# A hybrid decoder layer: recurrent rows first in the output projection, decay operands made during the input tiles, and the third down remainder behind the hidden halves

## The reference, cut to what matters

```python
h = x + concat(GatedDeltaNet(u), RG_LRU(u)) @ w_out      # u = rmsnorm(x); one projection u @ w_in feeds both
h = h + CrossAttn(rmsnorm(h), rmsnorm(mem))              # 4 heads, 256 memory tokens
h = h + MoE(rmsnorm(h))                                  # top 4 of 32 clamped-SwiGLU experts, D_FF = 1024
out = rmsnorm(h)

# GatedDeltaNet, 4 heads of 128: gcum = cumsum(g); decay = exp(gcum_t - gcum_s) below the diagonal
o = rmsnorm(o, dn_norm) * silu(z)                        # per head, then into the output projection
# one expert, for its tokens:
gt = min(x @ w_gate + b_gate, 7); up = clip(x @ w_up + b_up, -7, 7)
hid = (up + 1) * (gt * sigmoid(1.702 * gt)); y = hid @ w_down + b_down
```

## Time and profile before

| | us |
|---|---|
| median of three runs | 1742.11 |
| lowest, highest run | 1738.88, 1742.91 |
| profiled execution | 1739.81 |
| its span, first to last instruction | 1738.1 |

### The profile page before, as it was taken

How to read it: one execution, slowest core, us unless ns; L and a number is a source line. 1 busy time by engine, 2 the same in 40 slices (tenths; PEclk the granted TensorE clock), 3 DMA queues, 4 the chain that set the end, 5 groups by cost and what they waited for, 6 DMA issues and landing times.

```text
span 1738.1 us, 24427 instructions
## 1 busy us (share of the span) xinstructions
PE 1664.3 (96%) x8001; PEld 1367.4 (79%) x8001; DVE 1435.6 (83%) x1546; ACT 1273.5 (73%) x1456; POOL 496.4 (29%) x569
## 2 busy tenths in 40 slices
PE   5999899899899999999999999999999999999996
PEld 3778598787768888888888888888888888888885
DVE  3558796663348999999999999999999999999997
ACT  4554474454445788888888888888888888888885
POOL 3354461200023422223232232222322222222223
PEclk9999999999999999999999999999999999999999
DMA  7212200052024999999999999999999999999992
GB/s 253 103 37 93 84 1 2 25 194 97 8 102 194 375 363 383 380 355 384 362 385 383 353 376 368 382 380 356 369 376 379 375 364 363 379 381 361 375 355 107
DMA packets 53385, 476.19 MB, mean 274 GB/s; under 512 B 9991, under 2 KB 11144, under 8 KB 28770
## 3 DMA queue, kind: packets, MB, share of 16 engines
q1 hardware_dynamic: 42000, 450.69, 64.0%
q0 software_dynamic: 11152, 24.92, 6.3%
q10 hardware_dynamic: 194, 0.06, 0.0%
HBM read 461.24 MB, written 23.08 MB: 279 GB/s over the span
## 4 chain that ended last, share of the span: by engine, by line
PE 63%; DVE 16%; issue 13%; ACT 6%; POOL 1%; DMA 0%; ACTq 0%; DVEq 0%; POOLq 0%
PE ps L1569 19%; PE ps L1527 18%; PE ps L1147 10%; DVE wsp L1920 6%; PE ps L1318 4%; PE ps L1554 2%; ACT extra L1052 2%; PE ps L1502 2%; DVE extra L2109 1%; DVE extra L2107 1%; DVE wsp_b L1920 1%; DVE wf L1639 1%; PE ps L1252 1%; PE ps L1240 1%; PE ps L1409 1%
## 5 line engine op out<-in xcount | busy, mean ns | idle before, releaser
L1920 DVE TENSOR_TENSOR wsp<-ring,wsp 128x1024 fp32r<-128x1024 f32 x512 | 600.8, 1221 | 32.2 <-ACT wsp L1007 32.1
L1007 ACT ACTIVATE wsp<-ring 128x1024 fp32r<-128x1024 f32 x388 | 386.8, 1053 | 68.7 <-PE ps L1513 53.4
L589 POOL TENSOR_TENSOR guard<-guard 1x1 f32<-1x1 f32 x190 | 127.4, 670 | 772.3 <-ACT extra L1075 309.0
L1527 PE MATMUL ps<-wsp,x_hi 128*128 128x512 f32 x1152 | 308.1, 389 | 0.0
L1920 DVE TENSOR_TENSOR wsp_b<-ring,wsp_b 128x1024 fp32r<-128x1024 f32 x256 | 301.7, 1221 | 0.0
L1527 PEld LDWEIGHTS ps<-wsp,x_hi 128*128 128x128 f32 x1152 | 216.1, 188 | 45.7 <-issue 0.5
L1007 ACT ACTIVATE wsp_b<-ring 128x1024 fp32r<-128x1024 f32 x194 | 202.3, 1059 | 24.7 <-PE ps L1527 12.0
L1527 PE MATMUL ps<-wsp,x_lo 128*128 128x512 f32 x576 | 177.5, 389 | 0.0
L1639 DVE TENSOR_TENSOR wf<-ring,wf 128x1024 fp32r<-128x1024 f32 x64 | 81.3, 1273 | 106.0 <-ACT wf L707 106.0
L707 ACT ACTIVATE wf<-ring 128x1024 fp32r<-128x1024 f32 x80 | 84.3, 1056 | 112.0 <-PE ps L1147 62.5
L1147 PE MATMUL ps<-act_hi,wf 128*128 128x512 f32 x512 | 161.5, 397 | 2.6 <-DVE wf L1639 2.0
(11 more groups left out here) (382 smaller groups left out, 2951.9 us busy)
## 6 DMA issues: line engine op xcount, KB each, us to landing
ring<-in_w_gate_dram SPq DMA_DIRECT2D x32, 4096.0 KB, 15.0
ring<-in_w_up_dram SPq DMA_DIRECT2D x32, 4096.0 KB, 13.9
ring<-in_w_down_dram SPq DMA_DIRECT2D x32, 4096.0 KB, 13.0
ring<-in_w_in_dram SPq DMA_DIRECT2D x6, 2048.0 KB, 12.5
ring<-in_w_ckv_dram SPq DMA_DIRECT2D x4, 2048.0 KB, 10.2
ring<-in_w_out_dram SPq DMA_DIRECT2D x2, 2048.0 KB, 10.5
ring<-in_w_cq_dram SPq DMA_DIRECT2D x2, 2048.0 KB, 10.0
ring<-in_w_co_dram SPq DMA_DIRECT2D x2, 2048.0 KB, 10.0
```

Of the source, the lines that this page charges most:

```text
L589: return pool.tensor_tensor(guard[:, i:i + 1], guard[:, 0:1], guard[:, 0:1], ALU.mult)
L1007: act.activation(split_w(c, 0), ring[:, m, k], ACT.Copy).then_inc(hi_ready, 1)
L1527: last = pe.matmul(ps[:, 2 * j + i], xp[:, k * P:(k + 1) * P], split_w(c, part)[:, i * 512:(i + 1) * 512], start=False, stop=(k == KT - 1 ...
L1920: dve.tensor_tensor(split_w(c, 1), ring[:, (GM + c // KT) % 3, c % KT], split_w(c, 0), ALU.subtract).then_inc(lo_ready, 1)
```

## The change

Three places change. In the output projection all eight pieces of recurrent rows come first, for all four output groups; the rounding and remainders of the pieces move with them, the norm weight goes from a GpSimd instruction of its own into VectorE's multiply, both `fill_wait` go, and SP loads the memory rows after the scan's last output. The decay operands are made behind tiles 20, 21 and 22 into `y_m`, and their matmuls wait for their own bank's tile (18 to 21); the wait for tile 24 stands behind them. In the expert blocks `lo(18)` is issued behind both hidden halves.

```diff
@@ -284,8 +284,7 @@
         F_END = F_CO + N_CO
 
 
-        OUT_ORDER = ([(0, 0, 2), (0, 0, 3), (0, 1, 2), (0, 1, 3), (0, 0, 0), (0, 0, 1), (0, 1, 0), (0, 1, 1)]
-                     + [(1, n, kp) for n in range(2) for kp in (2, 3, 0, 1)])
+        OUT_ORDER = [(tp, n, kp) for kps in ((2, 3), (0, 1)) for tp in range(2) for n in range(2) for kp in kps]
         CV_ORDER = [(0, n, kp) for n in range(2) for kp in range(4)]
         CO_ORDER = [(tp, n, kp) for tp in range(2) for n in range(2) for kp in range(4)]
 
@@ -369,7 +368,7 @@
             sp.dma_start(w_ba[:], w_in[0].rearrange("(k p) n -> p k n", p=P)[:, :, C_BA:C_BA + 2 * H]).then_inc(ba_in, 16)
             for m in range(NF):
                 if m == W_CV:
-                    sp.wait_ge(dn_done, H)
+                    sp.wait_ge(o_done, 4 * NT)
                     sp.dma_start(chan[:, 0:4, :].rearrange("p a t -> p (a t)").rearrange("p (m d) -> p m d", m=MT),
                                  mem[0].rearrange("(m p) d -> p m d", p=P)).then_inc(mem_in, 16)
                 if m in FREE:
@@ -510,7 +509,6 @@
                 link(pool.tensor_tensor(chan[:, h], chan[:, h], q_m[:, h % 2], ALU.mult))
                 pool.tensor_copy(elast[:, 4 * h:4 * h + 4].unsqueeze(2), quart(q_m[:, h % 2])[:, :, P - 1:P]).then_inc(qexp_ready, 1)
                 pool.wait_ge(kk_evac, 4 * h + 1)
-                pool.wait_ge(gb_done, H)
                 if h >= 2:
                     pool.wait_ge(x1_ready, h - 1)
                 level_mask(0, h)
@@ -536,7 +534,6 @@
 
             for h in range(H):
                 pool.wait_ge(onorm_ready, h + 1)
-                link(pool.tensor_scalar(onrm(h), onrm(h), par[:, R_DN:R_DN + 1], None, ALU.mult))
                 pool.tensor_tensor(chan[:, 12 + h], chan[:, 12 + h], onrm(h), ALU.mult).then_inc(dn_done, 1)
 
 
@@ -881,22 +878,20 @@
             for h in range(H):
                 act.wait_ge(o_done, 4 * (NT - 1) + (h + 1 if h < 2 else H))
                 act.activation(onrm(h), ps[:, 4 + h], ACT.Square).then_inc(osq_ready, 1)
+                if h >= 2:
+                    piece_hi(F_OUT + h)
                 act.wait_ge(oss_done, h + 1)
                 act.activation(onrm(h), ps[:, h % 2], ACT.Sqrt, scale=1.0 / P, bias=eps_t).then_inc(orms_ready, 1)
-            piece_hi(F_OUT + 2)
-            piece_hi(F_OUT + 3)
-
             for h in range(H):
+                for i in ((), (4, 5), (6,), (7,))[h]:
+                    piece_hi(F_OUT + i)
                 act.wait_ge(dn_done, h + 1)
                 act.activation(act_hi[:, (6, 7, 4, 5)[h]], chan[:, 12 + h], ACT.Copy).then_inc(ah_ready, 1)
-                if h == 2:
-                    piece_hi(F_OUT + 4)
-            piece_hi(F_OUT + 5)
 
 
             s = NT
             memf = chan[:, 0:4, :].rearrange("p a t -> p (a t)").rearrange("p (m d) -> p m d", m=MT)
-            for i in range(6, 4 * HALF):
+            for i in range(2 * HALF, 4 * HALF):
                 piece_hi(F_OUT + i)
                 if i in (9, 11):
                     norm_rows(memf[:, s - NT], s, [(mem_in, 16)])
@@ -1170,10 +1165,10 @@
                     pe.matmul(ps[:, 6 + i % 2], ones[:], chan[:, 16 + i], start=True, stop=True).then_inc(l2_done, 1)
 
 
-            pe.wait_ge(tile_done, 24)
             for h in range(H):
+                pe.wait_ge(tile_done, 19 + h)
                 pe.wait_ge(gu_ready, h + 1)
-                pe.matmul(ps[:, h], ones[:], as_m[:, h % 2], start=True, stop=True).then_inc(gb_done, 1)
+                pe.matmul(ps[:, h], ones[:], y_m[:, h], start=True, stop=True).then_inc(gb_done, 1)
 
 
             def rg_gates(n):
@@ -1182,6 +1177,8 @@
                     if n > 0:
                         pe.wait_ge(ri_ready, 2 * (n - 1) + g + 1)
                     pe.matmul(ps[:, g], rgw[:, g, n], chan[:, 16 + n], start=True, stop=True).then_inc(gate_mm, 1)
+
+            pe.wait_ge(tile_done, 24)
 
             def head_products(h):
 
@@ -1340,12 +1337,11 @@
                 if h == 2:
                     mixer_out(1)
             pe.wait_ge(orms_ready, H)
-            fill_wait(24, 0)
             for i in range(2, 4 * HALF):
-                if i == 4:
-                    pe.wait_ge(onorm_ready, H)
-                    fill_wait(14, 4)
-                    pe.wait_ge(al_ready, A_DN)
+                if i in (4, 6):
+                    pe.wait_ge(onorm_ready, i - 2)
+                if i in (8, 9):
+                    pe.wait_ge(al_ready, A_DN + 2 * (i - 9))
                 if i == 14:
                     for m in range(MT):
                         transposes(NT + m, 2 * m)
@@ -1718,6 +1714,11 @@
                 if j == 3:
                     dve.wait_ge(gp_done, 1)
                     dve.tensor_copy(gp, ps[:, 7, 64:80]).then_inc(gp_ready, 1)
+                for h in {20: (0, 1), 21: (2,), 22: (3,)}.get(j, ()):
+                    if h == 0:
+                        dve.wait_ge(bias_out, 16 * 4)
+                    dve.tensor_tensor(quart(y_m[:, h]), tri[:].unsqueeze(1).to_broadcast([P, 4, P]),
+                                      g_t[:, 4 * h:4 * h + 4].unsqueeze(2).to_broadcast([P, 4, P]), ALU.mult).then_inc(gu_ready, 1)
                 if 11 <= j < 19:
                     i = j - 11
                     dve.wait_ge(norm_ready, i // 4 + 1)
@@ -1725,12 +1726,6 @@
                     dve.tensor_tensor(chan[:, i], chan[:, i], chan[:, 16 + i], ALU.mult).then_inc(qk_ready, 1)
 
 
-            for h in range(H):
-                dve.wait_ge(proj_done, 24)
-                if h >= 2:
-                    dve.wait_ge(gb_done, h - 1)
-                dve.tensor_tensor(quart(as_m[:, h % 2]), tri[:].unsqueeze(1).to_broadcast([P, 4, P]),
-                                  g_t[:, 4 * h:4 * h + 4].unsqueeze(2).to_broadcast([P, 4, P]), ALU.mult).then_inc(gu_ready, 1)
             for h in range(H):
                 dve.wait_ge(gb_done, h + 1)
                 dve.wait_ge(gp_ready, 1)
@@ -1825,17 +1820,14 @@
             for h in range(H):
                 dve.wait_ge(orms_ready, h + 1)
                 link(dve.reciprocal(onrm(h), onrm(h)))
-                dve.tensor_tensor(onrm(h), onrm(h), ps[:, 4 + h], ALU.mult).then_inc(onorm_ready, 1)
-                if h == 2:
-                    piece_lo(F_OUT + 2)
-                    piece_lo(F_OUT + 3)
+                dve.scalar_tensor_tensor(out=onrm(h), in0=onrm(h), scalar=par[:, R_DN:R_DN + 1], in1=ps[:, 4 + h],
+                                         op0=ALU.mult, op1=ALU.mult).then_inc(onorm_ready, 1)
+                for i in ((), (2, 3), (4, 5), (6, 7))[h]:
+                    piece_lo(F_OUT + i)
             for h in range(H):
                 dve.wait_ge(ah_ready, A_RG + h + 1)
                 k = (6, 7, 4, 5)[h]
                 dve.tensor_tensor(act_lo[:, k], chan[:, 12 + h], act_hi[:, k], ALU.subtract).then_inc(al_ready, 1)
-                if h == 2:
-                    piece_lo(F_OUT + 4)
-            piece_lo(F_OUT + 5)
 
             def add_resid(g, done, ready, t, n, bank):
 
@@ -1845,13 +1837,12 @@
 
             s = NT
             g = 0
-            for i in range(4, 4 * HALF):
-                if 6 <= i:
-                    piece_lo(F_OUT + i)
+            for i in range(2 * HALF, 4 * HALF):
+                piece_lo(F_OUT + i)
                 if i in (9, 11):
                     recip_rms(s + i // 2 - 4)
                 tp, n, kp, final = pair_of(F_OUT + i - 1)
-                if i > 4 and final:
+                if final:
                     for b in range(2):
                         add_resid(g, out_mm, h1_ready, 2 * tp + b, n, OUT_BANKS[tp, n][b])
                         g += 1
@@ -2094,7 +2085,7 @@
 
                 dve.wait_ge(sg_ready, n + 1)
                 dve.tensor_tensor(gs, ps[:, 0:2, :].rearrange("p b f -> p (b f)"), gs, ALU.mult).then_inc(gs_ready, 1)
-                for c in range(13, 19):
+                for c in range(13, 18):
                     lo(c, n * SPLIT + (c + 1))
 
                 for i in range(2):
@@ -2107,6 +2098,7 @@
                     dve.tensor_scalar(up[:, hs], ps[:, 2 + i], 8.0, -6.0, ALU.min, ALU.max).then_inc(up_ready, 1)
                     dve.wait_ge(up_ready, n * 2 + (i + 1))
                     dve.scalar_tensor_tensor(out=hid[:, hs], in0=gs[:, hs], scalar=CLIP, in1=up[:, hs], op0=ALU.min, op1=ALU.mult).then_inc(hid_ready, 1)
+                lo(18, n * SPLIT + 19)
                 for i in range(2):
                     dve.wait_ge(hidhi_ready, n * 2 + (i + 1))
                     dve.tensor_tensor(hid_lo[:, i * 512:(i + 1) * 512], ps[:, 2 + i], hid_hi[:, i * 512:(i + 1) * 512], ALU.subtract).then_inc(hidlo_ready, 1)
```

## The result

The changed kernel takes **1722.9 us** (median of four runs, 1721.8 to 1723.8); the kernel before took 1741.6 beside it (four runs, 1738.9 to 1742.9). The ratio is 0.9894, with a 95% interval from 0.9877 to 0.9912: 18.7 us faster. The profiled execution of after took 1723.8 us, its span is 1722.2, against 1739.8 and 1738.1 before; these two lie 15.9 apart, since before's was one of the quicker runs of its kernel and after's the slowest of its four.

A forecast was written before the change was run, and what follows sets the result against it. It took TensorE's chain as the bound: a wait for VectorE in every expert block and idle stretches in the decay stage and output projection. 4.9 + 8.2 + 5.4 = 18.5 us off gave 1722 us, range 1716 to 1729.

The forecast's parts named there:

- Part 1: Decay stage: operands made beside the input tiles let the decay subtraction start earlier, gain 4.9 us, from below 2.7.
- One mark of being wrong: Input tiles: the prediction called itself wrong if tiles 21 to 23 came later than in the kernel before.
- Part 2: Output projection: recurrent rows first and fills removed shorten the way to the memory keys, gain 8.2 us, bounds 4.2 and 8.4.
- 309.8: Output projection, before's clock: remainder of piece 5 ends, from 307.5 plus 1.05 for rounding and 1.2 for the remainder.
- 5.44 + 1.7 - 0.2: Output projection from piece 6: two pieces fewer (5.44), no half clock (1.7), more stall from the memory rows' normalisation (0.2).
- Part 3: Expert blocks: moving the third down remainder gains 0.17 us a block, 5.4 us over 32 blocks, bounds 0 and 15.
- longer than 0.2 us for hid_lo: Expert blocks: the prediction called itself wrong if TensorE's L1569 waited longer than 0.2 us for hid_lo.
- (a): Expert loop, moved stall: hid_lo takes all the bubble gave, only parts 1 and 2 count, 13.1 us, 1728; chance 0.16.
- (b): Expert loop: the bubble closes whole, 28 us in all, 1712; chance 0.09.
- (c): Output projection: without fills the clock falls again after the 1.9 us pause, 1.7 less, 16.8 in all, 1725; chance 0.08.
- (d): Expert loop: a stretched or extra remainder delays hid_lo, TensorE waits 0.97 longer a block, 18 us slower, 1758; chance 0.03.
- (e): After the output projection: a stage waits for something of fixed time, leaving 5.4 us of gain, 1735; chance 0.04.

The follow-up runs named there:

- e2: The kernel before with only the decay operands made during the input tiles: 1735.4 us, ratio 0.9971.
- e8: The kernel after with GpSimd's gate multiply cut to 8 of 512 columns, one run: 56.73 us from scan's end to memory keys, against 57.81 in after.
- e1: The kernel before with only the third down remainder moved behind both hidden halves: 1733.6 us, ratio 0.9962.
- e6: e4 with the load of the next expert's bias rows issued by SyncE instead of GpSimd: 1718.8 us, ratio 0.9882.
- e9: e4 with ScalarE's rounding of weight piece 21 moved behind the first hid_hi, bias load on GpSimd: 1713.6 us, ratio 0.9839.
- e4: The kernel after with the third down remainder moved one place further, behind the first hid_lo: 1792.8 us, ratio 1.0311.

## Why the prediction was right

Forecast 1722.0 us (1716 to 1729), measured 1722.9. The sum of 18.5 us stands against 18.7 by the medians; two of its three terms came out as worked out and the one for the output projection was 1.4 too large. That the sums lie 0.2 apart is luck: the profiled pair differs by 15.9.

**Part 1, 4.9 us: right.** The subtraction begins where the last tile's multiply ends, and comes 4.9 us nearer to the last projection matmul, in after and alone in e2. The four operations beside the tiles cost nothing: the last projection matmul ends 0.47 earlier, not later. The upper bound for stretching (4.6 us) wasn't touched. One tile operation beside them did stretch, the L1710 at 168.05 with 2.62 us, as its like did before. One mark of being wrong was crossed: of the tiles 21 to 23, tile 22 came 0.37 later. It cost nothing, since the pause before the last tile took it up (1.45 us instead of 2.90).

**Part 2, 8.2 us: the mechanism right, the size 6.8.** The forecast steps hold up to piece 2 (301.8 on the clock of before, 296.4 on after's; it started at 296.43). The one that failed is "309.8", the end of the remainder of piece 5. On after's clock that is 304.4, and the remainder ended at 305.63. Its price, 1.2 us, was taken from the loop, where no multiply of GpSimd runs beside it; here a pair takes 3.45 instead of 2.35. Piece 6 therefore started 26.05 us after the scan's end instead of 24.75, and piece 4 too had to wait. From piece 6 to the memory keys the forecast was 5.44 + 1.7 - 0.2 = 6.94 us of gain and 6.83 came (31.76 instead of 38.59). The gain of 1.25 at piece 6 became 310.95 - 284.90 - 26.00 = 0.05 of loss, and -0.05 + 6.83 = 6.8. e8 gives 1.08 of the 1.4 back; there piece 6 starts 24.99 us after the scan's end, 0.24 past the forecast, and what that 0.24 is wasn't taken apart. The stall of the memory rows' normalisation was 0.34, not 0.86. And the term of 1.7 for the half clock came out because the profile of before had that fall. e2 has the same code there and no fall, so beside it the new order gives 63.02 - 57.8 = 5.2 us; the term is a gain in some executions, and the prediction took it as certain.

**Part 3, 5.4 us: right, to the hundredth of a period.** 0.16 to 0.17 was forecast, 0.17 came in after and 0.18 in e1. The table of blocks follows the forecast step by step. The hidden transposes gain 0.38, and 0.10 more as their restart goes (0.75 becomes 0.65): the 0.48. The matmuls with hid_lo start 0.28 earlier and lose 0.11 to the restart (0.72 for 0.61): the 0.17. The mark "longer than 0.2 us for hid_lo" was crossed, 8.7 / 32 = 0.27, but it was set on the wrong row: 0.27 is what the weight load waited, while TensorE's own list has no such entry.

**The rivals.** (a) and (b) fall with the period; e6 and e9 show that the rest of the bubble could be had, 0.10 from hid_lo and 0.20 from hid_hi. (c) falls with the granted clock, which stayed at the higher level after the pauses of 1.38 and 1.72 us:

```profile
303.54:308.24 4.70, 4.70 (x21) 3.91 (x22) 4.70 (x2) 1.82 (x3) 1.00 (x1) 1.00 0.00 0
310.95:315.65 4.70, 4.70 (x21) 3.88 (x22) 4.70 (x6) 1.70 (x2) 1.00 (x1) 1.00 0.00 0
```

That is no rule for short pauses. The prediction found no case of one in the trace of before, but there is one: TensorE fell to the lower level at 553.1 behind pauses of 1.35 and 0.99 us. In after it fell at 464.56 behind pauses of 1.30 and 0.74.

(d) did not come; but a slower loop was nearer than the 3% given it, by a mechanism that the prediction did not name. GpSimd's small instructions already stood longer in after than before, 1096 ns in the mean instead of 670, and the bias had some 8 us to spare, 9 before. e4 went over that edge. (e) falls: all that the first two parts gave up to the memory keys was still there at the first of the matmuls of queries and memory keys (L1398 at 451.71 before, L1394 at 439.52 after).

## What to carry to other kernels

When an instruction is moved, price it by rows in which the same neighbours run: a remainder that cost 1.2 us in the loop cost 2.3 beside GpSimd's multiply. A fall of the clock read in one trace is no sure term of a sum: look for it in a second profile of the same code. When VectorE's pauses are closed, look at what GpSimd has queued, its DMA issues above all, for those pauses may be when it runs; a load that must be in time is safer on a queue that VectorE can't hold up. And in a loop whose bubble is a chain of short hand-overs, each place in the chain can be worked out to a tenth of a microsecond from one block's rows, but the next link has to be moved as well before TensorE runs without a wait.

## What the runs showed of the hardware that was not expected

- A GpSimd instruction on one element stood 11.62 us while VectorE ran remainders (two inputs in SBUF) one behind the other, and ended 0.05 us after VectorE's last. It did not get its turn at the ends of the ten remainders ahead of that one; in the output projection GpSimd's multiply did, at the end of the first of two. In e9 such an instruction stood 3.30 us and ended where VectorE's next remainder began 0.01 us after the one ahead, not 0.08 before its end. What decides it wasn't settled.
- When GpSimd had its turn first, VectorE's remainder was the one to stand: 2.31 instead of 1.22 us.
- The pause ahead does not by itself tell whether TensorE falls to its lower clock level. At the same place of the same code a pause of 3.55 us was followed by a granted clock of 0.64 (before) and one of 3.54 by 1.00 (e2). Pauses of 1.38 and 1.72 us were followed by 1.00, and in the same trace a fall came behind pauses of 1.30 and 0.74 (after, 464.56).
- The same 16 KB load from GpSimd's queue took 8.5 to 10.0 us from issue to landing in the blocks of after, 12.6 to 14.0 in the late blocks of e4 and in e9. What makes it longer wasn't tried.
